# Chunk-wise start of each layer for three tiles instead of two, shift columns in pairs, eleven tiles projected from x, and border squares added on GpSimd

## What is computed

```python
for l in range(2):
    sh1, sc1, g1, sh2, sc2, g2 = split(silu(c) @ w_ada[l] + b_ada[l])
    h = rms_norm(x, norm1_g[l]) * (1.0 + sc1) + sh1
    x = x + g1 * parallel_mixers(h, w_in[l], ...)   # attention branches A, B, C, gates, w_out
    h = rms_norm(x, norm2_g[l]) * (1.0 + sc2) + sh2
    x = x + g2 * peer_ffn(h, ...)                   # top-16 of 128x128 experts, 8 heads
```

## Time and profile before

| | |
|---|---|
| median of three runs | 2184.11 us (2183.80 to 2184.19) |
| the profiled execution, its own time | 2182.88 us |
| span of the profiled execution | 2181.1 us |
| mean granted TensorE clock | 0.996 |
| TensorE busy | 2151.9 us, 99% |
| VectorE busy | 1680.4 us, 77% |
| ScalarE busy | 1233.9 us, 57% |
| GpSimd busy | 245.7 us, 11% |
| read from HBM | 424.99 MB, 195 GB/s |

### The profile page before, as it was taken

The page is one execution under the profiler, slowest core; times in us unless marked ns, Lnnn a source line. Parts: engine busy times, 40 slices in busy tenths (PEclk is TensorE's granted clock), DMA queues, the critical chain, the costliest instruction groups (busy, mean ns, idle before and its releaser), DMA issues.

```text
span 2181.1 us, 43026 instructions
## 1 busy us (share of the span) xinstructions
PE 2151.9 (99%) x15008; PEld 1989.8 (91%) x15008; DVE 1680.4 (77%) x3258; ACT 1233.9 (57%) x2168; POOL 245.7 (11%) x298
## 2 busy tenths in 40 slices
PE   6999999999999999999999999999999999999999
PEld 5889999999999988888888899999999999888887
DVE  8777777889499956777577878788886997567765
ACT  5656575444577655555566565644455776555554
POOL 0210000000166400000002100000002662000000
PEclk8999999999999999999999999999999999999999
DMA  9466655555533367787665666455555334687864
GB/s 352 156 223 229 204 188 173 182 182 182 184 122 110 125 193 260 258 253 231 192 202 176 221 231 206 162 183 183 179 177 175 115 116 144 200 272 258 254 211 171
DMA packets 115440, 427.29 MB, mean 196 GB/s; under 512 B 12816, under 2 KB 13072, under 8 KB 113680
## 3 DMA queue, kind: packets, MB, share of 16 engines
q1 hardware_dynamic: 115344, 426.08, 58.2%
HBM read 424.99 MB, written 1.05 MB: 195 GB/s over the span
## 4 chain that ended last, share of the span: by engine, by line
PE 96%; DVE 2%; ACT 1%; DMA 1%; issue 0%; SPq 0%; ACTq 0%; DVEq 0%
PE pj L1453 18%; PE pj L1455 18%; PE pj L1454 18%; PE wk L1453 11%; PE wk L1455 11%; PE wk L1454 11%; PE wk L1814 5%; PE wk L1583 1%; PE wk L1560 1%; DMA arena<-in_front 1%; PE wk L1576 1%; PE wk L1522 1%; DVE arena L878 0%; PE wk L1743 0%; ACT hi L496 0%
## 5 line engine op out<-in xcount | busy, mean ns | idle before, releaser
L873 DVE TENSOR_TENSOR lo<-raw,hi 128x1024 fp32r<-128x1024 f32 x683 | 843.3, 1236 | 417.7 <-ACT hi L496 412.1
L496 ACT ACTIVATE hi<-raw 128x1024 fp32r<-128x1024 f32 x683 | 721.4, 1057 | 470.9 <-PE wk L1455 341.5
L1453 PE MATMUL pj<-mov_hi,hi 128*128 128x256 f32 x3008 | 867.8, 288 | 1.8 <-DVE x L1204 1.3
L1455 PE MATMUL pj<-mov_hi,lo 128*128 128x256 f32 x3008 | 851.5, 283 | 0.0
L1454 PE MATMUL pj<-mov_lo,hi 128*128 128x256 f32 x3008 | 850.9, 283 | 0.0
L1453 PEld LDWEIGHTS pj<-mov_hi,hi 128*128 128x128 f32 x3008 | 577.0, 192 | 10.9 <-issue 8.3
L1454 PEld LDWEIGHTS pj<-mov_lo,hi 128*128 128x128 f32 x3008 | 576.5, 192 | 0.1
L1455 PEld LDWEIGHTS pj<-mov_hi,lo 128*128 128x128 f32 x3008 | 575.9, 191 | 0.0
L1453 PE MATMUL wk<-hi,mov_hi 128*128 128x512 f32 x1024 | 398.5, 389 | 0.0
L1454 PE MATMUL wk<-lo,mov_hi 128*128 128x512 f32 x1024 | 398.4, 389 | 0.0
L1455 PE MATMUL wk<-hi,mov_lo 128*128 128x512 f32 x1024 | 398.4, 389 | 0.0
(11 more groups left out here) (207 smaller groups left out, 1896.1 us busy)
## 6 DMA issues: line engine op xcount, KB each, us to landing
raw<-in_stream SPq DMA_DIRECT2D x684, 512.0 KB, 3.4
arena<-in_ada SPq DMA_DIRECT2D x72, 512.0 KB, 4.8
onehot_a<-in_ada SPq DMA_DIRECT2D x24, 512.0 KB, 4.3
arena<-in_front SPq DMA_DIRECT2D x8, 1024.0 KB, 14.8
arena<-in_taba SPq DMA_DIRECT2D x2, 1536.0 KB, 8.7
arena<-in_keys SPq DMA_DIRECT2D x2, 1024.0 KB, 5.5
x<-in_xT SPq DMA_DIRECT2D x1, 1024.0 KB, 14.8
arena<-in_mix SPq DMA_DIRECT2D x2, 512.0 KB, 4.2
```

What stands on the lines that cost most here:

```text
L496: nc.scalar.activation(hi[j % SPLIT][:, :], raw[j % RAW][:, :], ACT.Copy).then_inc(hi_done, 1)
L873: nc.vector.tensor_tensor(lo[j % SPLIT][:, :], raw[j % RAW][:, :], hi[j % SPLIT][:, :].bitcast(f32), ALU.subtract).then_inc(lo_done, 1)
L1453: pe.matmul(out, w_h, m_h, start=first, stop=False)
L1455: return pe.matmul(out, w_l, m_h, start=False, stop=last)
```

## The change

- `FLIGHT = 3`: tiles 0, 1 and 2 run side by side, each chunk of u1 for all three. Tiles 2 and 3 go to two banks of wk (`u_bank`). SP issues three raw tiles, not two, ahead of the front transfers; VectorE splits tile 2 between the front modulations, and ScalarE's head of tile 2 stands ahead of its wait for x.
- The shift columns of layer 0 are set pair by pair of chunks, each after its two modulations, and release u1's chunks two at a time. In layer 0 the squares of chunk k stand ahead of chunk k's products.
- `N_U = 11`: tiles 0 to 10 are projected from u1. `U_OUT_AT` gives VectorE's steps for `u_scaled`, `H1_AT` those for h1. `U_FREE` gives what tiles 3 to 5 wait for.
- The root moves into ScalarE's step 0, between head(3) and head(4); VectorE's split of tile 4 moves from step 1 to step 0.
- At the border ScalarE alternates head of u1 and square, VectorE alternates x and u1's rest. GpSimd adds the eight squares in a chain of seven additions, and TensorE sums them with one matmul behind the three tiles.
- u1 lies at slot 12 of the arena instead of 78; the small tile grows from 96 to 102 columns.

```diff
-U_AT = (78, 24)
+U_AT = (12, 24)
...
-H1_AT = ((0, 1, 2), (3,), (4,), (5,), (6,), (7,), (), ())
-N_U = 7
+H1_AT = ((), (0,), (1,), (2,), (3,), (4,), (5, 6), (7,), (), (), (), ())
+N_U = 11
+FLIGHT = 3
+U_OUT_AT = {1: (0,), 2: (1,), 3: (2, 3), 4: (4,), 5: (5,), 6: (6,), 7: (7,), 9: (8,), 10: (9,), 11: (10,)}
+U_FREE = {3: 2, 4: 3, 5: 4}
...
+        def u_bank(t):
+            return wk[:, t - 2, :] if t in (2, 3) else pj[t % 2]
...
@@ SP @@
-            for j in range(2):
+            for j in range(FLIGHT):
                 sp.dma_start(raw[j][:, :], stream[j]).then_inc(raw_loaded[j], 16)
...
@@ GpSimd @@
+                if l:
+                    for k in range(1, KC):
+                        wait_alone(pool, sq_ready, 2 * KC * l + k + 1)
+                        if k > 1:
+                            wait_alone(pool, sq_total, (KC - 1) * (l - 1) + k - 1)
+                        nc.gpsimd.tensor_tensor(sq[:, 0, :], sq[:, 0, :], sq[:, k, :], ALU.add).then_inc(sq_total, 1)
...
-                    wait_alone(pool, out_free, l * OUTS + (t0 + 4 + 2))
+                    if t0 < N_U:
+                        wait_alone(pool, u_out, l * N_U + t0 + 4)
+                    else:
+                        wait_alone(pool, out_free, l * OUTS + (t0 + 4 + 2))
...
@@ ScalarE, loop over t @@
-                    head(L0 + (t + AHEAD), t + AHEAD)
+                    if t != 1:
+                        head(L0 + (t + AHEAD), t + AHEAD)
+                    if t == 0:
+                        first_root()
+                        head(L0 + (AHEAD + 1), AHEAD + 1)
...
@@ ScalarE, border @@
-                    first_norm(l + 1, link)
+                    act.wait_ge(amp_ready, l + 2)
+                    for k in range(KC):
+                        act.wait_ge(x_ready, (l + 1) * KC + (k + 1))
+                        u_heads(l + 1, k)
+                        square(k)
...
@@ VectorE, start @@
-            front(0, 8)
+            front(0, 4)
+            rest_of(2, 2)
+            front(4, 8)
...
+            for pair in range(KC // 2):
+                front(KC + 2 * pair, KC + 2 * pair + 2)
+                if pair == 0:
+                    dve.wait_ge(front_done, N_TURNED)
+                    nc.vector.tensor_tensor(mod[:, MS1:MS1 + 1], wk[:, 3, 0:1], par_all[:, 0, MS1:MS1 + 1], ALU.add)
+                    dve.sem_inc(late_used, N_TURNED)
+                at, end = MS1 + 2 * pair + (1 if pair == 0 else 0), MS1 + 2 * pair + 2
+                dve.wait_ge(late_used, KC + 2 * pair + 2)
+                slink(nc.vector.tensor_tensor(mod[:, at:end], mod[:, at:end], par_all[:, 0, at:end], ALU.add))
+                shift_columns(u1, MS1, slink, 2 * pair, 2 * pair + 2).then_inc(u_ready, 2)
...
@@ VectorE, loop over t @@
-                    if 0 < t <= N_U:
-                        u_scaled(t - 1)
+                    for n in U_OUT_AT.get(t, ()):
+                        u_scaled(n)
...
-                        rest_of(L0 + AHEAD, AHEAD)
+                        for j in range(AHEAD, AHEAD + 2):
+                            rest_of(L0 + j, j)
                         dve.wait_ge(rstd_ready, 2 * l + 1)
...
-                    if t:
+                    if t > 1:
                         rest_of(L0 + (t + AHEAD), t + AHEAD)
...
@@ VectorE, border @@
+                    if k and l + 1 < DEPTH:
+                        u_rest(l + 1, 0, u1, k - 1).then_inc(u_ready, 1)
...
@@ TensorE @@
+                def sum_of_squares():
+                    pe.wait_ge(sq_total, (KC - 1) * l)
+                    pe.matmul(wk[:, 5, 0:SEQ], ones, sq[:, 0, :], start=True, stop=True).then_inc(ss_ready, 1)
...
+                pe.wait_ge(lo_done, L0 + FLIGHT)
+                pe.wait_ge(out_free, l * OUTS + 2)
                 for k in range(KC):
+                    if l == 0:
+                        squares(k)
                     pe.wait_ge(u_ready, 2 * KC * l + k + 1)
-                    for t in range(2):
-                        last = product(pj[t][:, 0:COLS], *chunk(t, k), u1[:, 0, k, :], u1[:, 1, k, :], k == 0, k == KC - 1)
+                    for t in range(FLIGHT):
+                        last = product(u_bank(t)[:, 0:COLS], *chunk(t, k), u1[:, 0, k, :], u1[:, 1, k, :], k == 0, k == KC - 1)
                         if k == KC - 1:
                             last.then_inc(tile_done, 1)
+                if l:
+                    sum_of_squares()
-                for t in range(2, N_U):
+                for t in range(FLIGHT, N_U):
                     early_pieces(t)
-                    project_u(L0 + t, t, t, t % 2, u1, None).then_inc(tile_done, 1)
+                    project_u(L0 + t, t, U_FREE.get(t, t + 1) - 1, u_bank(t), u1, None).then_inc(tile_done, 1)
```

More of the change, by code:

```diff
@@ L139, in trunk @@
         gain = sb("gain", [P, 2])
-        small = sb("small", [P, 96])
+        small = sb("small", [P, 80 + 2 * N_U])
         routes = sb("routes", [P, 2, SEQ], f32r)
@@ L370, in _ @@
                 sp.dma_start(ada_front[:, f, :], front_dram[:, f, :]).then_inc(front_loaded[j], 16)
-            for j in range(2, RAW):
+            for j in range(FLIGHT, RAW):
                 sp.dma_start(raw[j][:, :], stream[j]).then_inc(raw_loaded[j], 16)
@@ L546, in link, with first_root @@
                     act.wait_ge(act_step, n_link[0])
+                def first_root():
+                    act.wait_ge(ss_ready, 2 * l + 1)
+                    link(nc.scalar.activation(rstd1, wk[:, 5, 0:SEQ], ACT.Ln, bias=eps, scale=1.0 / D))
+                    nc.scalar.activation(rstd1, rstd1, ACT.Exp, scale=-0.5).then_inc(rstd_ready, 1)
                 def second_root():
@@ L899, in scales, with shift_columns @@
                     link(nc.vector.tensor_scalar(gain[:, n:n + 1], par[:, g:g + 1], HD ** -0.5, None, ALU.mult))
[L901 to L905 removed]
+            def shift_columns(u, at, link, k0=0, k1=KC):
+                shifts = mod[:, at + k0:at + k1].unsqueeze(2).to_broadcast([P, k1 - k0, 2])
+                head_of, rest_in = u[:, 0, k0:k1, SEQ:COLS], u[:, 1, k0:k1, SEQ:COLS]
+                link(nc.vector.tensor_copy(head_of, shifts))
+                return nc.vector.tensor_tensor(rest_in, shifts, head_of.bitcast(f32), ALU.subtract)
             def u_rest(l, n, u, k):
@@ L1474, in _ @@
                     for k in range(KC):
-                        last = pe.matmul(wk[:, 1, tile:tile + 1], ada_front[:, n, k * P:(k + 1) * P], c_silu[:, k:k + 1],
+                        last = pe.matmul(wk[:, 3, tile:tile + 1], ada_front[:, n, k * P:(k + 1) * P], c_silu[:, k:k + 1],
                                          start=k == 0, stop=k == KC - 1)
@@ L1480, in _, with squares @@
                 L0 = l * TILES
-                def squares(n, sq, k):
-                    pe.wait_ge(sq_ready, 2 * KC * l + (n * KC + k + 1))
-                    last = pe.matmul(wk[:, 0, 0:SEQ], ones, sq[:, k, :], start=k == 0, stop=k == KC - 1)
+                def squares(k):
+                    pe.wait_ge(sq_ready, k + 1)
+                    last = pe.matmul(wk[:, 5, 0:SEQ], ones, sq[:, k, :], start=k == 0, stop=k == KC - 1)
                     if k == KC - 1:
                         last.then_inc(ss_ready, 1)
+                def sum_of_squares():
+                    pe.wait_ge(sq_total, (KC - 1) * l)
+                    pe.matmul(wk[:, 5, 0:SEQ], ones, sq[:, 0, :], start=True, stop=True).then_inc(ss_ready, 1)
                 def project_u(t, j, o, bank, u, ready, between={}):
@@ L1497, in project_u @@
                             between[k]()
-                        last = product(pj[bank][:, 0:COLS], *chunk(j, k), u[:, 0, k, :], u[:, 1, k, :], k == 0, k == KC - 1)
+                        last = product(bank[:, 0:COLS], *chunk(j, k), u[:, 0, k, :], u[:, 1, k, :], k == 0, k == KC - 1)
                     return last
@@ L1514, in project @@
                     return last
-                for k in range(KC):
-                    squares(0, sq, k)
                 def norms(n, region, first, size):
```

65 lines of the change are left out of this document (16 added, 49 removed).

## The result

| | before | after |
|---|---|---|
| median of the runs, side by side | 2183.95 us | 2204.31 us |
| their range | 2183.78 to 2184.19 | 2202.68 to 2207.65 (four runs) |
| the profiled execution, and its span | 2182.88, 2181.1 us | 2207.65, 2205.8 us |

The changed kernel takes 1.0095 times as long, with an interval of 1.0078 to 1.0113: +20.4 us. Forecast was 2195.8 us, +11.7, with a range from 2189 to 2204, so the direction was right, the size was too small by about 9 us, and the median lies 0.3 us above the range.

What follows compares the result with a forecast made beforehand. TensorE, busy 99% of the span, was taken as the bound. Norms and scores later in both layers, 3.8 + 3.1 + 1.7 + 3.1 = +11.7 us, gave 2195.8 us; the range was 2189 to 2204.

Steps and rivals of the forecast that it cites:

- Both waits: TensorE stands ahead of the norms and ahead of the scores in each layer, about 4.7 and 3.3 us.
- The chain from the end of Exp to the norms: VectorE's and ScalarE's steps from the root to branch A's norms, 16.5 us.
- Norms in layer 0: Branch A's norms, ahead of tile 7, start at 57.8 against 53.99: +3.8 us; in layer 1 +1.7 us.
- VectorE waiting for the end of tile 6: Ahead of the norms, steps 4 to 7 scale tile t itself, so `u_scaled(6)` waits for tile 6's end; 0.40 us.
- The starts: Start of tile 3 in each layer: -0.9 us in layer 0 (41.3), -3.9 us in layer 1 (1111.9).
- its worst bound 34: Layer 0's start: slow clock lasting to 34 us, which puts the start of tile 3 at 43.
- GpSimd's add: Layer 1's start: each of seven chained 128x256 adds of squares priced at 1.14 us, from the nearest row.
- the 0.4 us that the sum had: Layer 1's start: TensorE waits 0.4 us for the adds, which end at 1111.4, before tile 3.
- GpSimd decides: Rival at layer 1's start: adds over 1.13 us make TensorE wait; at 1.5 us each, 2198.3 us; 8%.
- the granted clock: TensorE's clock, taken as 1.00 throughout after the start, so the new waits cost only their length.
- the clock stood as a rival: Rival: the clock falls to half level in the new waits, once per layer, 6.6 us more, 2202.4 us; 13%.
- a sum above 2199: Sign: if the first wait is there but the time exceeds 2199 us, look at the clock and at GpSimd.

Runs made afterwards that it cites:

- The second attempt: Changed kernel with scalings in old steps, h1's chunks later, head(4) ahead of the root, square ahead of head(9), values' copy ahead of head(11): 2180.75 us.
- the square ahead: Changed kernel with ScalarE's square of branch A ahead of the heads of h1's chunks 5 and 6 in step 6: 2199.84 us.
- both layers: Changed kernel with scalings in old steps, h1 later, square ahead of h1's chunks, head(4) ahead of root; GpSimd adds squares in layer 0 too: 2188.33 us.
- columns at once: Changed kernel, reordered (old scaling steps, later h1, earlier square and head(4)), with layer 0's squares first and shift columns after the last modulation: 2191.44 us.
- steps put back: Changed kernel with only VectorE's scaling table restored, step t scaling tile t - 1 for all eleven tiles: 2190.91 us.

## Why the prediction was right in its chain, and which step failed

**The place and the chain: right.** Both waits stand where they were forecast, are released by what was forecast, and measure 4.4 us (4.7) and 3.5 us (3.3). The chain from the end of Exp to the norms, 16.5 us in the forecast, is 16.6 in both layers. Norms in layer 0: +3.7 and +4.5 in the two profiles (+3.8), in layer 1 +2.1 in both (+1.7). What was named as the reason, VectorE waiting for the end of tile 6, is not what decides at the norms: VectorE gets there 0.9 us late by itself, and with the table put back the norms start as late as before. The table decides at the scores: put back, it removes the second wait; alone, on a kernel that is in time, it makes it anew.

**The starts: layer 1 right, layer 0 about half of the forecast gain.** In layer 1 tile 3 began 1123.80 - 1112.39 = 11.4 us after the transposes against 15.43 before: -4.0 (-3.9). The forecast had also said what becomes of it: in the change's own order it is lost inside the norms' wait. The second attempt collects it. In layer 0 tile 3 began at 41.85 and 41.07 us in the two profiles (41.3; 42.23 before). In the ten profiles that have the change's own start it lies between 41.07 and 42.78, 41.8 in the mean: 0.4 us earlier than in the one profile of the kernel before, not 0.9. Two things move it from execution to execution: when the turned tile has landed (23.3 to 24.2 us), and when the half level ends, about 31 to 34 us by the products' durations, where the sum had 31 and its worst bound 34.

**GpSimd's add: mis-sized, without effect.** The nearest row was taken, 1.14 us, whose second operand comes from the small tile; the plain add is 0.74. TensorE didn't wait the 0.4 us that the sum had. The rival "GpSimd decides" is out.

**The step that failed is the granted clock.** The sum held it at full level over four waits of 3.3 to 4.7 us, and the clock stood as a rival at 13%, with 6.6 us. It measured 7.4 us and is the excess: 11.7 + 7.4 = 19.1 of 20.4, the rest being the waits' small differences and about 1 us behind the last scores that no run assigns. That the rival's 6.6 us come near to 7.4 is luck: it had 3.3 us once in each layer, and what was found is 1.7 to 2.4 us at each of four waits.

What misled was a single row, the 2.05 us wait of the kernel before that passed at full level. It was taken as if it bounded waits twice as long. The forecast said that nothing lay between it and the 13.9 us wait that did lower the clock, but that long wait had more to tell. It begins at 8.1 us, and these are two windows of the kernel before inside it:

```profile
11.00:11.50 0.50, 0.00 (x0) 0.00 (x0) 0.50 (x1) 0.00 (x0) 0.00 (x0) 1.00 1.06 442
...
12.00:12.50 0.50, 0.00 (x0) 0.00 (x0) 0.50 (x1) 0.00 (x0) 0.00 (x0) 0.50 1.08 459
```

The clock was down less than 4 us into the wait, and the forecast's own first wait was 4.7 us. With that row a fall was the likelier case at the first waits and an open one at the second, and the range had to reach well beyond 2204. The forecast did name the place to look, the clock, for a sum above 2199 with the first wait in place.

**What is settled and what isn't.** Shown: the clock's share, by filling the waits; the table's share, which is the second wait with its clock, from both sides; the adds' worth. The first wait is shown to hang on the chain from the root, and to go when h1's chunks, the square and head(4) are all moved; what each of these is worth alone is known for the chunks ahead of the square only (1.35 us). Open: the 2.2 us wait at L1600 in the first profile, which has no releaser. Shortly before it VectorE had stood 2.02 us for a tile of the modulation matrix, whose issue on SP had taken long:

```profile
1210.90 1.97 SPq L395 DMA_DIRECT2D arena<-in_ada  x1
```

Waits like it, of 2.2 to 2.4 us at the same line, were in the profiles of "the square ahead", "both layers" and "columns at once", and not in the other eight. In each of the three VectorE had stood 2.0 to 2.2 us for such a tile. But the long issue isn't common to them: it was 1.77 us in "columns at once" and 0.43 us, as usual, in the other two. In the first profile the wait and the fall of the clock behind it (0.79 over 8 us, 1.7 us) come to 3.9 us, of the 5.0 by which that execution is above the lowest of its kernel, 2202.68; no experiment was made on it.

## What to carry to other kernels

Price a new wait of the engine that bounds the kernel twice: its length, and the half level behind it. Here 3.5 to 4.4 us of waiting cost another 1.7 to 2.4, and a kernel that did useless work in the wait was 7.4 us faster. When the longest row that passed is shorter than the wait you forecast, don't hold the clock at full level: look inside the next longer wait for the moment at which it falls. When operations move to later steps of an in-order engine, follow every piece that stands behind them in those steps, up to the first instruction that the bounding engine waits for; three of the experiments missed their number by 4 to 11 us by pieces in those steps that had not been followed. And a gain at one point of the order is worth only what arrives at the next point at which the engines meet.

## What the hardware showed that was not expected

**Waits that bring the clock down.** Over the thirteen profiles of this study, every wait of TensorE of 1 us or more between 26 and 1250 us that began at full clock, with the mean granted clock of the 8 us that follow its end (a fall shows as 0.70 to 0.80):

| length of the wait, us | waits | followed by a fall |
|---|---|---|
| 1.0 to 1.5 | 3 | 0 |
| 1.8 | 8 | 2 |
| 2.0 to 2.4 | 8 | 5 |
| 3.0 to 3.1 | 2 | 1 |
| 3.4 to 4.4 | 13 | 13 |

The length alone doesn't decide below 3.4 us: the same wait of 1.83 us of the same program passed in one execution and not in another, and 2.02 us brought a fall where 2.05 passed. (One of the five in the third row, the 2.12 us wait of "steps put back", follows another of 2.00 us by 3 us.) The Trainium skill (TensorE: Matmul & The Clock Gate, Part 1) puts the fall down to idle time. The longest waits here agree with it, and the seven falls behind waits of 1.8 to 2.4 us show that short ones aren't safe either.

**The recorded clock can miss a fall.** In six of the profiles the windows of the start read 1.00 where the products take their half-speed time. In the changed kernel's second profile:

```profile
29.54 0.42 PE L1475 MATMUL wk<-u,hi 128*128 128x258 f32 x1
```

```profile
28.00:30.00 2.00, 2.00 (x10) 1.92 (x10) 2.00 (x4) 0.04 (x1) 0.31 (x1) 1.00 0.98 412
```

In the first profile the same product takes 0.42 us too, and the window reads 0.50; at full clock it takes 0.28. Of the 60 runs of the kernel before that stand beside the experiments, 27 have a mean clock of 1.000 and 33 one of 0.995 or 0.996, and the median time of both is 2183.6 us. So check a granted clock against the durations of equal products. Behind the waits of the table the two agree; one wait of 1.93 us, at the start of "both layers", is left out of it because the products on both sides ran at half speed under a recorded 1.00.

**GpSimd and VectorE side by side.** One add of 128x256 by GpSimd: 0.73 us by itself, 1.5 us beside modulations of 128x1024; VectorE's modulation that starts during one 1.74 instead of 1.21, a subtraction of four columns 0.60 instead of 0.16.
